# A diagonal of 1/rms as TensorE's operand, and the last half tile of a norm squared in two pieces

## What is computed

```python
def rms_norm(x, g):
    xf = x.astype(jnp.float32)
    y = xf * lax.rsqrt(jnp.mean(xf * xf, axis=-1, keepdims=True) + EPS)
    return (y * g.astype(jnp.float32)).astype(x.dtype)

def first_block(x, ...):
    for l in range(DEPTH):
        if l % 2 == 0:
            x = x + even_mixer(rms_norm(x, even_norm[e]), ...)
        else:
            x = x + retention_mixer(rms_norm(x, odd_norm[o]), ...)
        x = x + conv_glu_ffn(rms_norm(x, ffn_norm[l]), w_up[l], ffn_conv_w[l], w_down[l])
    return x
```

## Time and profile before

| | |
|---|---|
| median of 3 runs | 1759.37 us (1759.12, 1759.37, 1761.56) |
| profiled execution, its own time | 1759.93 us |
| its span | 1758.1 us |
| PE busy | 1712.4 us, 97% of the span |
| DVE, ACT, POOL busy | 868.4, 487.3, 22.0 us |
| DMA | 542.42 MB, mean 309 GB/s |
| norm 1, end of the stage before to first matmul of the next | 127.86 to 132.73 us |
| norm 2 | 318.77 to 323.82 us |
| norm 3 | 521.93 to 526.47 us |
| norm 4 | 712.99 to 716.36 us |

### The profile page before, as it was taken

How to read it: one execution, slowest core, us unless ns; L and a number is a source line. 1 busy time by engine, 2 the same in 40 slices (tenths; PEclk the granted TensorE clock), 3 DMA queues, 4 the chain that set the end, 5 groups by cost and what they waited for, 6 DMA issues and landing times.

```text
span 1758.1 us, 23716 instructions
## 1 busy us (share of the span) xinstructions
PE 1712.4 (97%) x9704; PEld 1136.9 (65%) x9704; DVE 868.4 (49%) x1532; ACT 487.3 (28%) x747; POOL 22.0 (1%) x31
## 2 busy tenths in 40 slices
PE   7999999999999999999999999999999999999997
PEld 6979999987789999844444444347764444444443
DVE  5778777765658777623234233233653233232323
ACT  5555444443455444310000000013430000000001
POOL 0100000000000000000000000000000000000000
PEclk9999999999999999999999999999999999999999
DMA  9535557564545656889999999997379999999994
GB/s 372 192 120 168 188 171 236 182 196 158 184 144 168 200 167 234 319 366 418 424 426 423 429 425 425 425 419 294 146 309 405 426 424 425 424 426 426 428 423 205
DMA packets 116764, 542.42 MB, mean 309 GB/s; under 512 B 5689, under 2 KB 51905, under 8 KB 88641
## 3 DMA queue, kind: packets, MB, share of 16 engines
q1 hardware_dynamic: 116240, 539.75, 77.9%
q10 hardware_dynamic: 432, 1.39, 0.2%
HBM read 540.07 MB, written 1.05 MB: 308 GB/s over the span
## 4 chain that ended last, share of the span: by engine, by line
PE 87%; DMA 4%; DVE 4%; SPq 2%; ACT 1%; issue 1%; POOL 1%; DVEq 0%; ACTq 0%; POOLq 0%
PE PS L2062 23%; PE PS L2092 11%; PE PS L701 11%; PE PS L702 11%; PE PS L703 11%; PE PS L2016 6%; DMA work<-w_up 4%; PE PS L542 2%; SPq L2176 2%; PE PS L2044 2%; PE PS L2045 1%; DVE e_w_lo L736 1%; PE PS L2076 1%; PE PS L1859 1%; PE PS L1552 0%
## 5 line engine op out<-in xcount | busy, mean ns | idle before, releaser
L2062 PE MATMUL PS<-ring,work 128*64 128x512 f32 x1152 | 279.7, 593 | 0.6 <-DMA ring<-w_up 0.6
L2151 DVE SCALAR_TENSOR_TENSOR work<-PS,small,work 128x512 f32<-128x512 f32 x32 | 24.0, 751 | 405.7 <-PE PS L2062 405.7
L2062 PE MATMUL PS<-work 128*64 128x512 f32 x656 | 205.3, 595 | 0.0
L2062 PEld LDWEIGHTS PS<-ring,work 128*64 128x64 f32 x1152 | 91.4, 137 | 164.3 <-issue 164.1
L2092 PE MATMUL PS<-ring,work 128*64 128x512 f32 x576 | 160.2, 598 | 1.6 <-ACT work L2117 1.6
L2016 PEld LDWEIGHTS PS<-work,hs 128*128 128x128 f32 x1024 | 116.7, 192 | 27.5 <-issue 24.3
L2062 PEld LDWEIGHTS PS<-work 128*64 128x64 f32 x656 | 66.7, 138 | 92.0 <-issue 92.0
L2016 PE MATMUL PS<-work,hs 128*128 128x128 f32 x1024 | 122.8, 278 | 2.7 <-DVE work L1999 2.7
L2092 PE MATMUL PS<-work 128*64 128x512 f32 x368 | 124.3, 598 | 0.0
L2117 ACT ACTIVATE work<-PS 128x512 f32<-128x512 f32 x32 | 19.1, 598 | 334.8 <-PE PS L2076 334.8
L1243 DVE TENSOR_TENSOR r_w_lo<-ring,r_w_hi 128x1024 fp32r<-128x1024 f32 x64 | 78.1, 1224 | 63.6 <-ACT r_w_hi L1236 62.4
(11 more groups left out here) (370 smaller groups left out, 3438.6 us busy)
## 6 DMA issues: line engine op xcount, KB each, us to landing
ring<-w_gate SPq DMA_DIRECT2D x32, 2048.0 KB, 26.7
ring<-w_down SPq DMA_DIRECT2D x32, 2048.0 KB, 24.9
ring<-w_up SPq DMA_DIRECT2D x28, 2048.0 KB, 24.0
ring<-ffn_w_up SPq DMA_DIRECT2D x22, 2048.0 KB, 8.7
work<-w_gate SPq DMA_DIRECT2D x16, 2048.0 KB, 28.5
work<-w_down SPq DMA_DIRECT2D x14, 2048.0 KB, 21.0
work<-w_up SPq DMA_DIRECT2D x14, 2048.0 KB, 21.3
ring<-ffn_w_down SPq DMA_DIRECT2D x22, 1024.0 KB, 6.0
```

The source lines that it names most:

```text
L2062: last = nc.tensor.matmul(PS[CAP * e:CAP * (e + 1), what, :], xg[:, c, CAP * e:CAP * (e + 1)], chunk_of(w[e], c), start=(c == 0), stop=(c ...
```

## The change

In norms 1, 2 and 3 (`SCALED`) DVE no longer scales the tiles. It multiplies the identity with `rstd` of the tile (`scaled_ident`, 128x128, written into the first 128 columns of `hs`), and PE multiplies each chunk of `x` itself with that diagonal, an ordinary float32 matmul. So turning and scaling are one step. Six of the eight products of tile 0 come ahead of the idle matmuls, which are fewer; two (bank 3, which the residual still reads) come between those of tile 1. The diagonal of tile 0 is made inside `residual_dve`, ahead of the last add.

In norms 1 to 4 (`SHARED`) the last half of tile 1 is added in two pieces of 256 columns. ACT squares the first and makes all of the mean that is known by then (`ms_more`); DVE squares the second (`ss_end`) and makes the mean itself.

Two waits of PE on memsets of DVE are gone (`ev_zero`, `ml_zero`).

```diff
         SHARED = (1, 2, 3, 4)
+        SCALED = (1, 2, 3)
+        END = BANK // 2
+        def turn(t):
+            return hs[:, t, 0:P]
...
                 if k in SHARED and t == n == 1:
-                    act.wait_ge(E("n_square"), SHARED.index(k) + 1)
+                    act.wait_ge(E("n_first"), SHARED.index(k) + 1)
+                    half = slice(BANK, BANK + END)
                 else:
                     act.wait_ge(E(name), values[t, n])
-                    link(nc.scalar.activation(hs[:, t, half], x[:, t, half], ACT.Square, accum_out=ss[:, t, n:n + 1]))
+                link(nc.scalar.activation(hs[:, t, half], x[:, t, half], ACT.Square, accum_out=ss[:, t, n:n + 1]))
+                if k in SHARED and t == n == 1:
+                    nc.scalar.activation(ms_more, ss[:, t, 1:2], ACT.Identity, bias=ms_part[:, t:t + 1],
+                                         scale=1.0 / D).then_inc(E("n_part"), 1)
+                    continue
...
+        def scaled_ident(dve, k, t):
+            dve.wait_ge(E("n_rstd"), NT * k + t + 1)
+            nc.vector.tensor_scalar(turn(t), ident, rstd[:, t:t + 1], None, ALU.mult).then_inc(E("n_hs"), 1)
...
             if k in SHARED:
                 name, values = X_DONE[k]
+                end = slice(BANK + END, D)
                 dve.wait_ge(E(name), values[1, 1])
-                nc.vector.scalar_tensor_tensor(hs[:, 1, BANK:], x[:, 1, BANK:], 1.0, x[:, 1, BANK:], ALU.mult, ALU.mult,
-                                               accum_out=ss[:, 1, 1:2]).then_inc(E("n_square"), 1)
+                link(nc.vector.scalar_tensor_tensor(hs[:, 1, end], x[:, 1, end], 1.0, x[:, 1, end], ALU.mult, ALU.mult, accum_out=ss_end))
+                dve.wait_ge(E("n_part"), SHARED.index(k) + 1)
+                nc.vector.tensor_scalar(ms[:, 1:2], ss_end, 1.0 / D, ms_more, ALU.mult, ALU.add).then_inc(E("n_ms"), 1)
             for i, t in enumerate(tiles(k)):
+                if k in SCALED:
+                    if t == 1:
+                        scaled_ident(dve, k, t)
+                    continue
                 dve.wait_ge(E("n_rstd"), NT * k + i + 1)
...
-        IDLE = {1: (0, 14), 2: (4, 7), 3: (4, 7), 4: (4, 12)}
+        IDLE = {1: (4, 2), 2: (4, 3), 3: (4, 3), 4: (4, 12)}

         def norm_pe(pe, k):
+            if k in SCALED:
+                def turned(t, c):
+                    return nc.tensor.matmul(bank(c // 2)[:, (c % 2) * S + t * P:(c % 2) * S + (t + 1) * P], chunk(x[:, t, :], k, c), turn(t),
+                                            start=True, stop=True)
+                pe.wait_ge(E("n_hs"), NT * k + 1)
+                for c in range(DC - 2):
+                    turned(0, c)
+                idle(*IDLE[k])
+                pe.wait_ge(E("n_hs"), NT * k + 2)
+                for b in range(4):
+                    for c in (2 * b, 2 * b + 1):
+                        if b == 3:
+                            turned(0, c)
+                        last = turned(1, c)
+                    last.then_inc(E("n_tr"), 1)
+                return
...
-                    v = x[:, t, n * BANK:(n + 1) * BANK]
-                    nc.vector.tensor_tensor(v, v, bank(first_bank + n * NT + t), ALU.add).then_inc(E(name + "_add"), 1)
+                    v, out_ps = x[:, t, n * BANK:(n + 1) * BANK], bank(first_bank + n * NT + t)
+                    if k in SCALED and t == n == 1:
+                        scaled_ident(dve, k, 0)
+                    if k and t == n == 1:
+                        nc.vector.tensor_tensor(v[:, 0:END], v[:, 0:END], out_ps[:, 0:END], ALU.add).then_inc(E("n_first"), 1)
+                        v, out_ps = v[:, END:], out_ps[:, END:]
+                    nc.vector.tensor_tensor(v, v, out_ps, ALU.add).then_inc(E(name + "_add"), 1)
```

More of the change, by code:

```diff
@@ L219, in build @@
         ss, ms, rstd, ms_part = scratch(0, NT, 2), scratch(4, NT), scratch(6, NT), scratch(288, NT)
+        ms_more, ss_end = scratch(290, 1), scratch(291, 1)
         hss, hms, hrstd = scratch(8, NT, 16), scratch(40, NT, 16), scratch(72, NT, 16)
@@ L660, in build, with residual_dve @@
         OUT_BEFORE = {"even": 0, "ret": 2 * NT, "mla": 4 * NT}
-        def residual_dve(dve, name, before=0, units=0, first_bank=0):
+        def residual_dve(dve, name, before=0, units=0, first_bank=0, k=None):
             ps, ps_before = ("out_ps", OUT_BEFORE[name]) if name in OUT_BEFORE else (name + "_ps", 0)
@@ L806, in between @@
                     conv_chunk(2 * CONV_FIRST + 1 + i)
-            pe.wait_ge(E("ev_zero"), 2)
             heads_pe(pe, "ev", score, lambda h, t: v_t[:, t, h // 2 * P:(h // 2 + 1) * P],
@@ L907, in even_dve @@
                 other = slice((1 - i) * A_DIM, (2 - i) * A_DIM)
-                nc.vector.memset(kT[other, i, :, :], 0.0).then_inc(E("ev_zero"), 1)
+                nc.vector.memset(kT[other, i, :, :], 0.0)
             norm_dve(dve, link, 0, meanwhile)
@@ L965, in even_dve @@
             rest_part(dve, 0, GATE, 0, units.slot(), 1)
-            residual_dve(dve, "even", first_bank=4)
+            residual_dve(dve, "even", first_bank=4, k=1)
         IN_LOOP = 3
@@ L1210, in ffn_dve @@
                 rest_quarters(dve, units, 0, EARLY)
-            residual_dve(dve, "ffn", 4 * l)
+            residual_dve(dve, "ffn", 4 * l, k=2 + 2 * l)
         RET_UNITS = 16
@@ L1456, in ret_dve @@
             ffn_first_dve(dve, units, 1, GATE)
-            residual_dve(dve, "ret")
+            residual_dve(dve, "ret", k=3)
         def pool_load(units):
@@ L1655, in mla_pe @@
             values(0)
-            pe.wait_ge(E("ml_zero"), 2)
             pe.wait_ge(E("ml_qrT"), 2)
@@ L1750, in mla_dve @@
                 other = slice((1 - i) * M_ROPE, (2 - i) * M_ROPE)
-                nc.vector.memset(krT[other, i, :], 0.0).then_inc(E("ml_zero"), 1)
+                nc.vector.memset(krT[other, i, :], 0.0)
             for t in range(NT):
```

## The result

The changed kernel takes 1780.1 us (median of 4, 1779.16 to 1780.88), the kernel before 1759.24 on the same chip (4, 1758.18 to 1761.56): a ratio of 1.0117 with an interval of 1.0104 to 1.0130. It is 20.9 us slower, where +2.85 was forecast and 1765.0 was the upper end.

A forecast was written before the change was run, and what follows sets the result against it. TensorE (PE), holding 87% of the chain, was taken to bound the kernel. Norms 1 to 4 add 0.54 + 1.34 + 0.87 + 0.1 = +2.85 us, moving the median from 1759.37 to 1762.2 us; range 1759.2 to 1765.0.

The forecast's parts named there:

- Two rows for one fp32 product, so 0.22 a product: PE's products in norms 1 to 3: two rows each at the idle matmuls' 0.112 us a row.
- plus 1.1 us in each SCALED norm: Norms 1 to 3: ten products behind diagonal 1 take 2.3 us, where 1.20 passed before.
- +0.54, +1.34 and +0.87: Predicted net losses in us of norms 1, 2 and 3, up to PE's first matmul of the next stage.
- At nothing: ... the shorter idle runs, and two waits on memsets: Freed DVE time, fewer idle matmuls and two PE waits met long before were priced at zero.
- DVE idle behind tile 0's power in norm 2: Ahead of norm 2's last add, DVE waits 1.3 us for POOL's power of tile 0.
- Powers: POOL's powers take 0.55 us everywhere but in norm 4, standing still only while DVE holds SBUF.
- rival C: Norm 2's powers are slow by themselves: +1.1, so +3.95 us in all, 1763.3; chance 0.08.
- Norm 4: Not SCALED, only the two pieces: tile 0's scaling moves behind the sum and delays the power, +0.1 us.
- The dense part's loss passed on: Every microsecond lost ahead of the mixture-of-experts part reaches the end in full.
- D: Products in norms 1 to 3 cost what a transpose does: -0.4 us, 1759.0, no change; chance 0.12.
- B: The clock falls behind PE's gap in norm 2, costing 1.7 us: +4.5 in all, 1763.9; chance 0.12.
- if the clock column falls below 1.00 in a norm: Sign that would show the prediction wrong: granted clock under the 2.4 GHz level in a norm.

The follow-up runs named there:

- the kernel with contiguous chunks: Changed kernel with four idle matmuls fewer and retention's weights and gain laid out so norm 2's chunks are 128 neighbouring columns: 1767.53 us, ratio 1.0046.
- Pieces alone: Changed kernel with no norm scaled by a product; transposes, DVE scaling and idle counts as before, only the two pieces and DVE's mean left: 1759.62 us, ratio 1.0003.
- +7: Kernel before without the wait on the memsets, 9 idle matmuls for 7 in norm 2: 1766.97 us, ratio 1.0044.
- +15: Kernel before without the wait on the memsets, 11 idle matmuls for 7 in norm 2: 1767.67 us, ratio 1.0035.
- +23: Kernel before without the wait on the memsets, 11 and 9 idle matmuls for 7 and 7 in norms 2 and 3: 1767.75 us, ratio 1.0029.
- -1: Changed kernel with four idle matmuls fewer, PE's program one instruction shorter than in the kernel before: 1771.69 us, ratio 1.0066.
- 0: The kernel before itself, PE's program unmoved: 1759.24 us.
- +3: Kernel before without the wait on the memsets, 8 idle matmuls for 7 in norm 2: 1759.45 us, ratio 1.0003.
- +31: Kernel before without the wait on the memsets, 11, 9 and 14 idle matmuls for 7, 7 and 12 in norms 2 to 4: 1759.27 us, ratio 1.0006.
- the diagonal behind the adds: The kernel with contiguous chunks, with tile 0's diagonal made behind the last adds instead of ahead of them: 1769.09 us, ratio 1.0044.

## Why the prediction was wrong, point by point

**"Two rows for one fp32 product, so 0.22 a product"** is the step that failed. It took the pace from idle matmuls that read a contiguous identity, and the products read every eighth column. Measured: 0.467. The sum's "plus 1.1 us in each SCALED norm" came out at about +3.5 for the ten held products (4.68 less 1.2). The six early ones, which the prediction had hidden, ran past diagonal 1 with the idle matmuls behind them, by 0.93, 1.49 and 1.14 us in norms 1, 2 and 3. With 0.18 us by which diagonal 1 was late in each norm that is the whole of it: against +0.54, +1.34 and +0.87 the norms measured +4.02, +5.39 and +4.57. The Trainium skill (TensorE: Matmul & The Clock Gate, section Terms) had transposing four times faster for FP32; the prediction set it aside for the measured row, and for this operand the trace is with the page, 4.2. For contiguous operands it is with the row, a factor of two (the idle matmuls of the earlier trace rows, and norm 2 of the kernel with contiguous chunks). Both held in this case; the row was of another access pattern.

**"At nothing: ... the shorter idle runs, and two waits on memsets"** is the second that failed, and no rival had it. The sum has no term for the length of PE's program. The products, the shorter idle runs and one wait together moved it by 15 instructions, into a position at which it pauses 5.1 us at 1200 us, far behind the last edit. With the clock that falls behind it that is 6.0 us in the trace (4.57 and 1.44). That the position brings it is shown by the runs in both directions; that PE waits for its own program there is not.

**Steps that held.** DVE idle behind tile 0's power in norm 2: 1.61 against 1.3 (0.2 of the difference is that the third add ends that much before the last could start, but the gap was worth only 0.57 when it was taken out; diagonal 1 was ready at 4.27 and not 4.09). Powers: 0.55 in norms 1 to 3, twice in norm 2, where before the two took 2.26; in norm 4, where one still lies beside a scaling, 0.99. That is the contention read in the prediction, and rival C is out. Norm 4: +0.24 against +0.1 (from the start of the last add to PE's first product with the band matrix 3.58 us, 726.44 to 730.02, and 3.34 before). Pieces alone: nothing in the total, though not in their norms. The dense part's loss passed on: 14.22 in the four norms, 13.66 at norm 4's end. "In full" was not quite it. The 14.67 at the end of the first expert part hold 1.0 us more. Most of it comes from a wait of PE for weights, 0.68 us ahead of L2105 at 1172.82 and none before, in a stretch where the queues are full.

**The rivals.** D, a product as cheap as a transpose, lay on the wrong side. B's fall of the clock came behind the pause, and before that where B had it, in norm 2 behind the wait for diagonal 0, and the sign "if the clock column falls below 1.00 in a norm" came true (0.84). It cost 0.3 us and not 1.7, since the rows with a step of eight took 0.240 us at 0.50 and 0.238 at 1.00, and only the idle matmuls slowed (0.213 against 0.112). The same wait of 1.80 us in the kernel with contiguous chunks brought no fall, so such a gap can bring one and does not always, as B said. The range was made of bounds that all used the contiguous row, so it could not hold the result.

Nothing tried beats the kernel before. Even with contiguous chunks and the stall shortened norm 2 takes 6.01 us and not 5.05: ten products at 0.225 and a diagonal take PE to L1309 2.6 us behind the last power, where one scaling and eight transposes took 2.0. That is 0.6 of the 1.0; the rest lies ahead of that power.

## What to carry to other kernels

Price a matmul from a row that has its operands' strides, not only its shape and type: a fp32 product whose stationary or moving operand steps four or eight values took twice the time of a contiguous one, while transposes of the same chunks did not. When a total moves more than the places that were edited, read the chain for "issue" before an engine's first instruction behind a loop, and run the old kernel with harmless instructions added until it sits at the new one's position; with an effect of 0.4% that moves in and out, a small gain or loss of any edit must be checked at two positions before it is believed.

## What was not expected of the hardware

- The step of an fp32 operand: 0.112 us a row contiguous, 0.117 at two, 0.225 at four, 0.234 at eight; either operand alone brings it, both together bring no more (0.239). A one-row transpose of eighth columns takes 0.112.
- A row with a step of eight costs the same at both clocks, 0.240 us at 0.50 and 0.238 at 1.00; a contiguous one took 0.213 and 0.112 (distances between the starts of single rows in norms 2 and 3 of the changed kernel).
- PE's pause of 5.1 us at positions +7, +15 and +23 and not at -1, 0, +3 and +31, with the granted clock at 0.66 around and behind it in the changed kernel. A packet on the instruction queue begins 2.6 us ahead of PE's restart in all four kernels that have the pause.
- Between norm 4 and the first expert gather the granted clock falls for some microseconds, before the change too, but not equally long in all kernels. At +23 it stood so:

```profile
735.00:740.00 5.00, 5.00 (x25) 5.00 (x25) 4.35 (x29) 3.42 (x4) 0.00 (x0) 0.50 0.99 421
```

and before so:

```profile
735.00:740.00 5.00, 5.00 (x35) 5.00 (x34) 4.17 (x29) 3.50 (x4) 0.00 (x0) 0.72 0.97 414
```

A half is the 1.2 GHz level for the whole stretch. At +15, at +23, with pieces alone and with the diagonal behind the adds the first 32 matmuls of the gather took 5.36 to 5.47 us and not 3.84. Pieces alone has no pause, and at +7 there is a pause and 3.84, so the two do not go together. What decides the length of the fall stays open; it may be part of why the runs of one kernel spread over 5 to 9 us.
